# Two of the four weight-block sums by accumulating DMAs, and block products from the fourth tile pair of each feed-forward on

## What is computed

```python
def swiglu(x, w_gate, w_up, w_down):
    return (jax.nn.silu(x @ w_gate) * (x @ w_up)) @ w_down

for l in range(DEPTH):
    h = layer_norm(a * h + 0.5 * swiglu(h, ffn1_w_gate[l], ffn1_w_up[l], ffn1_w_down[l]), ln1_g[l], ln1_b[l])
    ...                                   # mixer: causal pooling beside gated linear attention, then layer_norm
    h = layer_norm(a * h + 0.5 * swiglu(h, ffn2_w_gate[l], ffn2_w_up[l], ffn2_w_down[l]), ln3_g[l], ln3_b[l])
```

## Time and profile before

| | |
|---|---|
| runs (3) | median 1961.26 us, 1959.46 to 1963.83 |
| profiled execution | 1958.71 us, its span 1957.0 us |
| mean granted TensorE clock | 0.967 of full |
| busy: TensorE, VectorE, ScalarE, GpSimd | 1886.8, 1232.3, 825.4, 446.2 us |
| matmuls | 14406 |

### The profile page before, as it was taken

One profiled execution on the slowest core, in us unless ns is written; L12 is line 12 of the kernel. 1 busy time (PEld: TensorE's weight loads), 2 busy tenths in 40 slices (PEclk: granted clock), 3 DMA queues, 4 the chain that ended last, 5 costly groups with the idle time before them and its releaser, 6 DMA issues.

```text
span 1957.0 us, 34609 instructions
## 1 busy us (share of the span) xinstructions
PE 1886.8 (96%) x14406; PEld 1802.3 (92%) x14406; DVE 1232.3 (63%) x1834; ACT 825.4 (42%) x1297; POOL 446.2 (23%) x200
## 2 busy tenths in 40 slices
PE   8999999989999999999999999999899999999996
PEld 8999999879898999999999999998797778899895
DVE  6728557667448837728487385577674488386475
ACT  4525435452125534525455254354431255345253
POOL 4030302332122240030521203023321221402113
PEclk9999999989898999999989999999898889999998
DMA  4333323321111332233323233232211113333232
GB/s 152 100 103 106 104 91 104 97 66 55 44 48 50 102 104 97 92 101 106 114 75 100 95 108 109 87 109 87 65 55 44 54 53 99 108 108 109 86 110 86
DMA packets 48828, 175.26 MB, mean 90 GB/s; under 512 B 5408, under 2 KB 5408, under 8 KB 48672
## 3 DMA queue, kind: packets, MB, share of 16 engines
q1 hardware_dynamic: 48240, 171.78, 28.0%
q10 hardware_dynamic: 432, 1.25, 0.2%
HBM read 170.92 MB, written 2.10 MB: 88 GB/s over the span
## 4 chain that ended last, share of the span: by engine, by line
PE 86%; DVE 9%; issue 2%; ACT 2%; DMA 1%; POOL 0%; DVEq 0%; ACTq 0%
PE PS L371 13%; PE PS L372 13%; PE PS L373 13%; PE PS L424 12%; PE PS L427 12%; PE PS L426 12%; PE PS L403 2%; PE PS L381 2%; PE PS L382 1%; PE PS L679 1%; PE PS L712 1%; DVE win L1533 1%; PE PS L524 1%; PE PS L710 1%; DVE qt L1488 1%
## 5 line engine op out<-in xcount | busy, mean ns | idle before, releaser
L330 POOL TENSOR_TENSOR w_lo<-raw,w_hi 128x1024 fp32r<-128x1024 f32 x172 | 431.3, 2511 | 1483.4 <-ACT w_hi L852 1058.8
L371 PE MATMUL PS<-h_hi,w_hi 128*128 128x264 f32 (+1 forms) x1238 | 370.2, 299 | 0.5 <-DVE h_lo L1134 0.2
L372 PE MATMUL PS<-h_lo,w_hi 128*128 128x264 f32 (+1 forms) x1238 | 369.7, 299 | 0.0
L373 PE MATMUL PS<-h_hi,w_lo 128*128 128x264 f32 (+1 forms) x1238 | 369.4, 298 | 0.0
L852 ACT ACTIVATE w_hi<-raw 128x1024 fp32r<-128x1024 f32 x240 | 215.1, 930 | 231.8 <-PE PS L373 179.1
L424 PE MATMUL PS<-v_hi,s_hi 128*128 128x264 f32 (+1 forms) x864 | 245.0, 284 | 6.1 <-DVE s_lo L1200 6.1
L371 PE MATMUL PS<-x_hi,w_hi 128*128 128x264 f32 (+2 forms) x796 | 245.2, 308 | 5.0 <-DVE ft L1526 4.9
L426 PE MATMUL PS<-v_lo,s_hi 128*128 128x264 f32 (+1 forms) x864 | 244.3, 283 | 0.0
L427 PE MATMUL PS<-v_hi,s_lo 128*128 128x264 f32 (+1 forms) x864 | 243.9, 282 | 0.0
L372 PE MATMUL PS<-x_lo,w_hi 128*128 128x264 f32 (+2 forms) x796 | 242.2, 304 | 0.0
L371 PEld LDWEIGHTS PS<-h_hi,w_hi 128*128 128x128 f32 x1238 | 233.0, 188 | 9.1 <-DVE h_lo L1134 1.6
(11 more groups left out here) (217 smaller groups left out, 4008.2 us busy)
## 6 DMA issues: line engine op xcount, KB each, us to landing
raw<-in_stream SPq DMA_DIRECT2D x316, 512.0 KB, 3.7
raw_first<-in_stream SPq DMA_DIRECT2D x4, 512.0 KB, 5.7
out_t<-X SPq DMA_DIRECT2D x8, 256.0 KB, 2.1
X<-in_x_t SPq DMA_DIRECT2D x7, 264.0 KB, 7.5
par<-in_params ACTq DMA_DIRECT2D x2, 480.0 KB, 3.6
X<-in_x_t ACTq DMA_DIRECT2D x1, 264.0 KB, 4.5
```

The lines of the kernel that those rows point to most:

```text
L330: nc.gpsimd.tensor_tensor(w_lo[:, slot, :], raw[:, slot % RAWS, :], w_hi[:, slot, :].bitcast(F32), ALU.subtract).then_inc(lo_done[slot], 1)
L371: nc.tensor.matmul(o, hi, rhs_hi[:, k, tok], start=first, stop=False)
L372: nc.tensor.matmul(o, hi, rhs_lo[:, k, tok], start=False, stop=False)
L373: return nc.tensor.matmul(o, lo, rhs_hi[:, k, tok], start=False, stop=last)
```

## The change

`CLASSIC` becomes 3, so that pair 3 of each feed-forward is fast: 19 fast pairs in each instead of 18. S1 and S3 are no longer made by VectorE. SyncE loads u.low twice over into two halves of a new buffer (`load_shared`, one DMA, the source repeated), and GpSimd issues two accumulating DMAs that add u.high to the one and g.low to the other (`add_other`). VectorE makes S2 and S4 into `s_more`. The up piece of a fast pair is loaded without its low half.

```diff
-CLASSIC = 4
+CLASSIC = 3
...
+FAST_GATES = {gate_piece(l, f, m) - 1: fast_index(l, f, m)
+              for l in range(DEPTH) for f in range(2) for m in range(CLASSIC, MT)}
+PHASE_FIRST = {fast_index(l, f, max(m0, CLASSIC)) for l in range(DEPTH) for f in range(2) for m0, _ in PHASES}
+SUMS_BEFORE = {max(n - 2, SLOTS + RAWS) if i in PHASE_FIRST else n: (i, n) for n, i in FAST_GATES.items()}
...
+            def load_shared(i, gate):
+                if i > 0:
+                    sp.wait_ge(S["s_lo_done"], 4 * max(i - 1, 1))
+                if i % FAST < 2 and i >= FAST:
+                    sp.wait_ge(S["o_acc"], 4 * ((i // FAST + 1) // 2))
+                shared = stream[(gate + 1) // RAWS, (gate + 1) % RAWS][:, 0:BLOCK]
+                sp.dma_start(s_two[:, i % 2, :, :], shared.rearrange("p (o c) -> p o c", o=1)
+                             .to_broadcast([P, 2, BLOCK])).then_inc(s_loaded[i % 2], 16)
             for n in range(SLOTS + RAWS, DEPTH * LAYER_PIECES):
+                if n in SUMS_BEFORE:
+                    load_shared(*SUMS_BEFORE[n])
                 wait_piece(sp, n - RAWS)
-                sp.dma_start(raw[:, n % RAWS, :], stream[n // RAWS, n % RAWS]).then_inc(raw_full[n % RAWS], 16)
+                part = slice(BLOCK if n - 1 in FAST_GATES else 0, PIECE)
+                sp.dma_start(raw[:, n % RAWS, part], stream[n // RAWS, n % RAWS][:, part]).then_inc(raw_full[n % RAWS], 16)
...
+            def add_other(i, gate):
+                pool.wait_ge(s_loaded[i % 2], 16 * (i // 2 + 1))
+                for j, n, part in ((1, gate + 1, slice(BLOCK, PIECE)), (3, gate, slice(0, BLOCK))):
+                    pool.dma_start(two_term(i, j), stream[n // RAWS, n % RAWS][:, part],
+                                   accum_op=ALU.add).then_inc(s_added[i % 2], 16)
             for n in range(SLOTS, DEPTH * LAYER_PIECES):
+                if n in SUMS_BEFORE:
+                    add_other(*SUMS_BEFORE[n])
                 if whole(n):
                     split(n)
...
-            def w_sums(i, gate, js):
...
+            def w_sums(i, gate):
+                g = raw[:, gate % RAWS, :]
+                wait_added(dve, i)
+                wait_raw(dve, gate)
+                if i > 0:
+                    dve.wait_ge(S["s_lo_done"], 4 * i)
...
+                V.tensor_tensor(s_more[:, 0, :], two_term(i, 1), g[:, 0:BLOCK], ALU.add).then_inc(S["s_sum_done"], 1)
+                dve.wait_ge(S["s_sum_done"], 2 * i + 1)
+                V.tensor_tensor(s_more[:, 1, :], s_more[:, 0, :], g[:, BLOCK:PIECE], ALU.add).then_inc(S["s_sum_done"], 1)
```

More of the change, by code:

```diff
@@ L77 @@
 FAST = MT - CLASSIC
-S_ORDER = (1, 3, 2, 4)
 V_ORDER = (3, 1, 2, 4)
@@ L191, in build @@
         with ExitStack() as s6:
-            s_sum = sb("s_sum", [P, 4, BLOCK], F32, s6)
+            s_two = sb("s_two", [P, 2, 2, BLOCK], F32, s6)
         acc_a = sb("acc_a", [P, HEADS, NCH, CH])
@@ L209, in build @@
             s_lo = sb("s_lo", [P, 4, BLOCK], F32R, s5)
+            sb("reserve_v_sum", [P, 4 * BAND * HALF - 8 * BLOCK], F32, s5)
+            s_more = sb("s_more", [P, 2, BLOCK], F32, s5)
         with ExitStack() as s2:
@@ L287, in build @@
         raw_full = [sem(f"raw_full{i}") for i in range(RAWS)]
+        s_loaded = [sem(f"s_loaded{i}") for i in range(2)]
+        s_added = [sem(f"s_added{i}") for i in range(2)]
         lo_done = [sem(f"lo_done{i}") for i in range(SLOTS)]
@@ L298, in wait_raw, with wait_added, two_term, summed_weights @@
             eng.wait_ge(raw_full[n % RAWS], 16 * ((n - SLOTS) // RAWS + 1))
+        def wait_added(eng, i):
+            eng.wait_ge(s_added[i % 2], 32 * (i // 2 + 1))
+        def two_term(i, j):
+            return s_two[:, i % 2, j // 2, :]
+        def summed_weights(i, j):
+            return two_term(i, j) if j % 2 else s_more[:, j // 2 - 1, :]
         def wait_stream(eng, l, idx):
@@ L841, in sum_high @@
             def sum_high(i, j):
-                act.wait_ge(S["s_sum_done"], 4 * i + S_ORDER.index(j) + 1)
+                if j % 2:
+                    wait_added(act, i)
+                else:
+                    act.wait_ge(S["s_sum_done"], 2 * i + j // 2)
                 if i > 0:
                     act.wait_ge(S[("p5_acc", "p6_acc", "p7_acc", "p3_acc")[j - 1]], i)
-                nc.scalar.activation(s_hi[:, j - 1, :], s_sum[:, j - 1, :], ACT.Copy).then_inc(S["s_hi_done"], 1)
+                if i % FAST == 0:
+                    act.wait_ge(S["v_lo_done"], 4 * (i // FAST) + 4)
+                nc.scalar.activation(s_hi[:, j - 1, :], summed_weights(i, j), ACT.Copy).then_inc(S["s_hi_done"], 1)
             def high_part(n, part):
@@ L1170, in v_low @@
                                 ALU.subtract).then_inc(S["v_lo_done"], 1)
-            def w_sums(i, gate, js):
[L1174 to L1191, removed]
+            def w_sums(i, gate):
[4 more added lines that the diff above has]
+                    dve.wait_ge(S["s_lo_done"], 4 * i)
+                if i % FAST == 0:
+                    dve.wait_ge(S["v_lo_done"], 4 * (i // FAST) + 4)
+                V.tensor_tensor(s_more[:, 0, :], two_term(i, 1), g[:, 0:BLOCK], ALU.add).then_inc(S["s_sum_done"], 1)
+                dve.wait_ge(S["s_sum_done"], 2 * i + 1)
+                V.tensor_tensor(s_more[:, 1, :], s_more[:, 0, :], g[:, BLOCK:PIECE], ALU.add).then_inc(S["s_sum_done"], 1)
             def raw_low(n, part):
@@ L1199, in sum_low @@
                 dve.wait_ge(S["s_hi_done"], 4 * i + j)
-                V.tensor_tensor(s_lo[:, j - 1, :], s_sum[:, j - 1, :], s_hi[:, j - 1, :].bitcast(F32),
+                V.tensor_tensor(s_lo[:, j - 1, :], summed_weights(i, j), s_hi[:, j - 1, :].bitcast(F32),
                                 ALU.subtract).then_inc(S["s_lo_done"], 1)
@@ L1230, in ffn @@
                             if m == CLASSIC - 2:
-                                w_sums(fast_index(l, f, CLASSIC), gate + 4, S_ORDER)
+                                w_sums(fast_index(l, f, CLASSIC), gate + 4)
                                 pair_low(gate + 4)
@@ L1241, in ffn @@
                         if follows:
-                            w_sums(i + 1, gate + 2, S_ORDER)
+                            w_sums(i + 1, gate + 2)
                         if after_fast:
@@ L1285, in ffn @@
                                             ALU.add).then_inc(S["down_evac"], 1)
[L1286 to L1289, removed]
+                        if mo == 5:
+                            w_sums(i, nxt)
                         elif mo == 6:
```

## The result

The changed kernel takes **1992.4 us** (1989.4 to 1998.9, 4 runs) where the kernel before takes 1961.0 beside it: ratio 1.0163, interval 1.0134 to 1.0192. That is slower, as forecast, but by 31 us where 6.8 were forecast, and outside the range. The profiled execution has a span of 1989.3 us, 32.3 more than before, at nearly the same mean clock (0.965 for 0.967).

A forecast was written before the change was run, and what follows sets the result against it. TensorE, busy 1886.8 of 1957.0 us, was taken as the bound. Saving 5.2, losing 4.9 at the feed-forwards' starts and 7.1 in the first fast pair gave +6.8 us on 1961.26: 1968.1 us, range 1959 to 1980.

The forecast's parts named there:

- What it removes: On TensorE, one classic pair in each feed-forward becomes a fast one: together 5.2 us less.
- The start of each feed-forward: VectorE is late for the first fast pair of each feed-forward: together 4.9 us more, 1.1 in each of three, 1.6 last.
- the locks: Second `v_lo` couples wait beside GpSimd subtractions that the change removes: 2.42 us instead of 4.63; 22.5 us cost if this stays.
- The stop in pair 0: Once, in the first feed-forward: pair 1's load waits for pair 0's sums, so TensorE stops; 7.1 us (4.9 to 10.2).
- Rival 3: After pauses in fast pair 0 TensorE's clock falls to half for 7 to 10 us, costing 2.4 to 3.4; chance a third.
- I take 0 for all of these: In fast pairs after the program's first, the 8.7 us chain of load and adds stays hidden and costs nothing.
- The limit of 12.9 us: In steady fast pairs, time from a sum's low part to VectorE's next sums before TensorE waits: 12.9 us for the chain.
- My upper bound: For the chain, 11.8 us: a 3.7 us load, then two 3.7 us transfers one behind the other, plus an issue each.
- rival 2: In steady fast pairs the chain of load and adds exceeds 12.9 us and becomes the bound; over 1980 us, chance 10%.
- its example of 15 us: With a 15 us chain a fast pair takes 11.3 us instead of 10.2: +65 over some 60 pairs, 2033 us.

## Why the prediction was wrong

- **What it removes** (-5.2): right. Four pairs are shorter, -5.6 by the trace; in the last feed-forward a fast pair takes 9.81, not 10.19.
- **The start of each feed-forward** (+4.9): right, +5.2. The second `v_lo` couple takes 2.42 us, as forecast from the locks in the earlier trace rows (the line now has 1214 to 1253 ns over all 16). The wait for the gate is 1.02 us for a forecast of 0.8; the wait for `s_lo` stayed 1.54, so the sum was met a little differently.
- **The stop in pair 0** (+7.1): the mechanism was right, the size came out at its upper bound. It cost 10.1. The chain took 11.3 us instead of 8.7 (load 4.6 for 3.7, adds from issue to landing 6.4 for 5.0, 0.3 from landing to issue that I had left out), so VectorE went on at 64.93, not 60.6. TensorE's two waits are 7.0 us; the rest is mostly the clock (the windows above). Rival 3 had that at 2.4 to 3.4 with a chance of a third.
- **"I take 0 for all of these"**, the steady pairs: this is the step that failed, +20.8 us, or 19.4 without the pair that the clock slowed. The three terms above measure +9.7 together where +6.8 was forecast, so slower was rightly forecast, and the time would have been in the range without this step. The limit of 12.9 us was right to a few tenths; the chain that I set against it was 8.7 and measures 13.2. The load takes 4.7 us, the first add is issued 0.3 after it lands and the second 0.54 after the first; the second lands 6.0 to 8.9 us after the first one's issue (median 7.9), with the weights of a pair (512 and 256 KB) loaded beside it. My upper bound, two transfers one behind the other and an issue each (11.8 for the chain), came from rows in which at most one other DMA ran beside a load: before, a weight load takes 3.6 us alone and 3.7 with one other. In the changed kernel such a load (512 or 256 KB) takes 3.6 alone and 5.7 with four others, an add 4.4 with one other and 6.9 with four (medians; the others are the DMAs that are under way at some time between its issue and its landing). So rival 2 came true in its mechanism, at 10% chance, and in a milder size than its example of 15 us. Its rule (two pairs per chain plus 7.5 us) gives 10.35 us a pair for 13.2, which is 0.16 over the free pace, where the trace has 0.40 (20.8 us over 52 pairs), since the chains vary and only the long ones count. The third buffer leaves 2.6 us of TensorE's 13.3 us of waits for the addition in PSUM, and more traffic beside the chain makes them 32.6, so here the cause is shown, from both sides.

The Trainium skill's page DMA: Bandwidth & Descriptors, in the section on the anatomy of a DMA, gives 2.6 us for a DMA of 256 KB that GpSimd issues, by its formula; the trace has a median of 5.9 for the accumulating ones and 5.5 for plain 256 KB loads beside them, and 4.6 and 5.2 for the program's first two adds, with one weight load beside them. The measurement decides: the formula would have made my error larger. The page SBUF — State Buffer, section Who interferes with whom, says that making descriptors does not hold up a `tensor_tensor`; the trace agrees: GpSimd issues for 1.0 us each, 132 us in all (the two of a pair overlap), and VectorE's sums take 691 ns, as before.

What stays open: the 1.4 us at the program's start come and go between kernels with and without the new DMAs and were not pursued; and with the chain hidden, `CLASSIC` 4 still shows 0.15% (0.06 to 0.23) over the kernel before, for which the trace offers 2.8 us of waits for GpSimd's splits, not tested by itself; its fast pairs take no longer in sum (1101.2 us for 1101.6).

## What to carry to other kernels

A chain that recurs has a limit (here: two pairs less the consumer's own work) and a length, and it is the length's share of other traffic that one gets wrong: take a transfer's time from a row in which the same neighbours run, and if the margin is only a third of the limit (4.2 of 12.9 here), put down a loss and not a zero. Once such a chain is the bound, each tenth counts once per period (here two pairs), and the cure is depth and an early issue (a third buffer, a queue in which it stands behind nothing) rather than a faster transfer. And work taken from an engine buys only what the bottleneck waits for it: nothing with `CLASSIC = 4`, some 7 us at the four starts with `CLASSIC = 3`. Count what it costs elsewhere first.

## What the runs showed that was not expected

- An accumulating DMA of 256 KB lands 5.9 us (median) after its issue and a plain load of 512 KB 3.7, but the neighbours account for part of this: plain loads of 256 KB beside such DMAs take 5.5, and adds with a single other DMA beside them 4.4.
- The place in a queue made 6.8 to 7.1 us (median; 8.2 in the block shown) of a 512 KB load issued right behind two weight loads, which takes 4.7 when it is issued some 4 us after them, with the same bytes in all.
- In one run the gate's low part made TensorE pause at the start of each feed-forward. After pauses of 2.07, 2.08 and 2.46 us the granted clock was at half from about a microsecond after the pause's end, or from its very end, for 3.4 to 6.8 us; after the fourth, of 2.00 us, it stayed at full.
